# Layer norms of a two-block network: statistics about the first group's mean, scale and shift folded into the operand, output stored by column blocks

## The reference

```python
for i in range(2):
    sh, sc, gt = modulation(c_lat, w_ada[i], b_ada[i], 3)   # cond vector times a 2048 x 6144 matrix
    u = x * (1.0 + sc) + sh
    y = even_mixer(u, ...) if i == 0 else odd_mixer(u, ...)  # end in "@ w_out", 2048 x 2048
    x = layer_norm_2(alpha * x + gt * y, ln_g[i], ln_b[i])   # alpha = 4 ** 0.25
return x

def layer_norm_2(x, g, b):
    mu = mean(x, -1); var = mean((x - mu) ** 2, -1)          # over the 2048 channels of a token
    return (x - mu) * rsqrt(var + 1e-5) * g + b
```

## Time and profile before

| | us |
|---|---|
| median of 3 runs | 3116.04 (3108.94 to 3119.6) |
| the profiled execution, whole | 3112.09 |
| its span, first to last instruction | 3110.3 |
| TensorE busy | 2884.9 (93%) |
| VectorE busy | 1744.7 (56%) |
| ScalarE busy | 1024.1 (33%) |
| DMA, mean over the span | 145 GB/s |

### The profile page before, as it was taken

One profiled execution on the slowest core, in us unless ns is written; L12 is line 12 of the kernel. 1 busy time (PEld: TensorE's weight loads), 2 busy tenths in 40 slices (PEclk: granted clock), 3 DMA queues, 4 the chain that ended last, 5 costly groups with the idle time before them and its releaser, 6 DMA issues.

```text
span 3110.3 us, 36197 instructions
## 1 busy us (share of the span) xinstructions
PE 2884.9 (93%) x12539; PEld 2245.0 (72%) x12539; DVE 1744.7 (56%) x2683; ACT 1024.1 (33%) x1583; POOL 15.8 (1%) x26
## 2 busy tenths in 40 slices
PE   6999999989999979599999999999999699999995
PEld 3478877666788757378878777776788488888883
DVE  6855764444687555354427466473866576325343
ACT  3032223333332253322234435342322332234224
POOL 0000000000000000000000000000000000000000
PEclk9999999999999989799999999999999899999997
DMA  9975642212466346165522222233666274333331
GB/s 348 336 224 189 190 142 79 61 58 68 136 203 204 132 152 235 61 221 189 191 80 89 75 81 75 81 101 117 208 218 214 73 249 147 95 96 101 122 109 54
DMA packets 225492, 451.14 MB, mean 145 GB/s; under 512 B 23752, under 2 KB 29338, under 8 KB 221004
## 3 DMA queue, kind: packets, MB, share of 16 engines
q1 hardware_dynamic: 222548, 440.80, 43.2%
q0 software_dynamic: 2304, 8.39, 0.8%
q10 hardware_dynamic: 504, 0.17, 0.0%
HBM read 422.01 MB, written 27.30 MB: 144 GB/s over the span
## 4 chain that ended last, share of the span: by engine, by line
PE 83%; DVE 5%; ACT 4%; issue 2%; DMA 2%; DVEq 1%; ACTq 1%; SPq 1%; PEldq 0%; PEld 0%
PE ps L1142 20%; PE ps L1144 20%; PE ps L1143 20%; PE ps L1234 4%; PE ps L1151 2%; PE ps L1153 2%; PE ps L1152 2%; PE ps L1512 2%; PE ps L1195 2%; PE ps L1382 1%; DMA a_raw<-in_w_ada 1%; PE ps L1390 1%; PE ps L1121 1%; PE ps L1543 1%; PE ps L1546 1%
## 5 line engine op out<-in xcount | busy, mean ns | idle before, releaser
L1142 PE MATMUL ps<-op_hi,w_hi 128*128 128x512 f32 (+2 forms) x2928 | 1174.4, 401 | 56.4 <-DVE op_lo L1676 17.9
L1143 PE MATMUL ps<-op_lo,w_hi 128*128 128x512 f32 (+2 forms) x2928 | 1152.2, 394 | 0.0
L1144 PE MATMUL ps<-op_hi,w_lo 128*128 128x512 f32 (+2 forms) x2928 | 1152.1, 393 | 0.0
L1570 DVE TENSOR_TENSOR w_lo<-w_raw,w_hi 128x512 fp32r<-128x512 f32 (+2 forms) x640 | 421.4, 661 | 597.7 <-ACT w_hi L658 391.4
L1142 PEld LDWEIGHTS ps<-op_hi,w_hi 128*128 128x128 f32 (+1 forms) x2928 | 559.0, 191 | 193.3 <-issue 28.4
L1144 PEld LDWEIGHTS ps<-op_hi,w_lo 128*128 128x128 f32 (+1 forms) x2928 | 558.2, 191 | 119.1
L1143 PEld LDWEIGHTS ps<-op_lo,w_hi 128*128 128x128 f32 (+1 forms) x2928 | 559.7, 191 | 112.3 <-issue 1.9
L658 ACT ACTIVATE w_hi<-w_raw 128x512 fp32r<-128x512 f32 x464 | 292.5, 632 | 905.0 <-PE ps L1144 732.3
L1593 DVE SCALAR_TENSOR_TENSOR acc<-a_raw,vec,acc 128x512 f32<-128x512 f32 x525 | 381.7, 746 | 22.8 <-DMA a_raw<-in_w_ada 22.8
L634 ACT ACTIVATE w_hi<-w_raw 128x512 fp32r<-128x512 f32 (+2 forms) x240 | 134.5, 565 | 357.0 <-PE ps L1144 301.9
L1151 PE MATMUL ps<-w_hi,op_hi 128*128 128x512 f32 x384 | 152.6, 397 | 14.5 <-DVE w_lo L1570 14.5
(11 more groups left out here) (221 smaller groups left out, 2331.9 us busy)
## 6 DMA issues: line engine op xcount, KB each, us to landing
a_raw<-in_w_ada SPq DMA_DIRECT2D x216, 512.0 KB, 4.0
w_raw<-in_w_in_e SPq DMA_DIRECT2D x160, 512.0 KB, 4.6
w_raw<-in_w_in SPq DMA_DIRECT2D x96, 512.0 KB, 4.8
arena<-in_w_ada SPq DMA_DIRECT2D x72, 512.0 KB, 7.1
w_raw<-in_w_in_o SPq DMA_DIRECT2D x64, 512.0 KB, 3.8
w_raw<-in_w_out SPq DMA_DIRECT2D x32, 512.0 KB, 4.9
w_raw<-in_w_out_e SPq DMA_DIRECT2D x32, 512.0 KB, 4.9
w_raw<-in_w_out_o SPq DMA_DIRECT2D x32, 512.0 KB, 3.6
```

Source lines behind the costliest of these rows:

```text
L1142: mm(dst, hi[:, cols], B.op_hi[:, k, 0:tok], start=first, stop=False)
L1143: mm(dst, hi[:, cols], B.op_lo[:, k, 0:tok], start=False, stop=False)
L1144: last = mm(dst, lo[:, cols], B.op_hi[:, k, 0:tok], start=False, stop=last_t)
L1570: V.tensor_tensor(B.w_lo[:, c % RING, 0:width], B.w_raw[:, c // 2 % RAW, c % 2, 0:width], B.w_hi[:, c % RING, 0:width].bitcast(f32), ALU.s ...
```

## The change

- **Statistics beside the groups.** When `wo2` 0 (and `wo3` 0) is evacuated, its four tiles are added and summed on TensorE during group 1 (one ones-product at t = 3). The mean of those 512 channels per token, negated, is the shift. At t = 5 VectorE adds it to tiles 0 to 3; the residuals of groups 1 to 3 get it when they are scaled, now at t = 13 of their group, so all of Y is held about that mean. During group i (1 to 3) ScalarE squares the four tiles of group i - 1 and VectorE adds the tiles and the squares into sums. After group 3 only its own four tiles are left: TensorE adds the stored sum and four tiles, and the stored squares and four tiles' squares, ten ones-products, and the variance is E[y^2] - E[y]^2.
- **No centring pass.** A tile is normed by a multiply with the inverse deviation r and a subtraction of mean * r.
- **Folding.** For the operand of `xp`, gain, bias, scale and shift are combined into one scale and one shift per channel, so ScalarE makes the operand from the normed tile by one Identity. Gain and bias of the stream itself are applied one tile at a time, four tiles behind the operand (`stream_gain`), the last four after tile 15.
- **Output.** The end goes by blocks of 512 channels: gains of block j + 1, then copies of block j, one store of [512 tokens x 512 channels] per block from four buffers.
- The last three modulation parts move from `xp` 0 to 2 to `xp` 1 to 3. ScalarE's loops over `wo2` and `wo3` groups, and VectorE's over `wo3` groups, are written out step by step.

Core of the diff (hunks for bookkeeping left out; blank lines too):

```diff
     part = 8
     for start, count in ((first["f"], 7), (first["gb"], 5), (first["ck"], 2), (first["r"], 6),
-                         (first["egb"] + 1, 8)):
+                         (first["egb"] + 1, 5), (first["xp"] + 1, 3)):
...
+SHIFT_AT, SHIFTED_AT, SQUARED_AT, SCALED_AT = 3, 5, 9, 13
...
-    for t in range(NT):
-        sp.wait_ge(sem("out_rows"), t + 1)
-        sp.dma_start(B.out[0, t * P:(t + 1) * P, :], at(AT_OUT, 2, D)[:, t % 2, :]).then_inc(sem(f"out_done_{t % 2}"), 16)
-    for k in range(2):
-        sp.wait_ge(sem(f"out_done_{k}"), 16 * NT // 2)
+    for j in range(4):
+        sp.wait_ge(sem("out_rows"), j + 1)
+        cols = slice(j * GC, (j + 1) * GC)
+        sp.dma_start(B.out[0].rearrange("(t p) d -> p t d", p=P)[:, :, cols], at(AT_OUT, NT, D)[:, :, cols])\
+            .then_inc(sem("out_done"), 16)
+    sp.wait_ge(sem("out_done"), 64)
...
+    def group_squares(n, t):
+        g = GROUPS[n]
+        if g["name"] not in ("wo2", "wo3") or t != (SHIFTED_AT + 2 if g["i"] == 1 else SHIFTED_AT) or not g["i"]:
+            return
+        k, j = ("wo2", "wo3").index(g["name"]), g["i"] - 1
+        act.wait_ge(sem("centred"), 7 * k + j + 1)
+        if j:
+            act.wait_ge(sem("squares_added"), 3 * k + j)
+        Act(at(AT_SQ, 2048), Y[:, 4 * j:4 * j + 4, :].rearrange("p a b -> p (a b)"),
+            ACT.Square).then_inc(sem("tile_squared"), 1)
...
+    def last_squares(k):
+        act.wait_ge(sem("squares_added"), 3 * k + 3)
+        for t in range(4):
+            act.wait_ge(sem("centred"), 7 * k + 4 + t)
+            Act(at(AT_SQ, 4, S)[:, t, :], Y[:, 12 + t, :], ACT.Square).then_inc(sem("tile_squared"), 1)
...
+    def deviation(k):
+        act.wait_ge(sem("variance"), k + 3)
+        r = at(AT_RSTD, S)
+        Act(r, r, ACT.Ln, bias=B.eps[:, 0:1])
+        nc.scalar.drain()
+        Act(r, r, ACT.Exp, scale=-0.5).then_inc(sem("deviation"), 1)
...
+    def stream_gain(k, t):
+        g, b = (VEC[v] + 16 * k + t for v in ("ln_g", "ln_b"))
+        return Act(Y[:, t, :], Y[:, t, :], ACT.Identity, scale=B.vec[:, g:g + 1], bias=B.vec[:, b:b + 1])
...
+    def normed_operand():
+        n = first_use(5)
+        act.wait_ge(sem("w_used"), GROUPS[n]["kc"])
+        for t in range(KT):
+            act.wait_ge(sem("tile_normed"), t + 1)
+            if t >= 4:
+                act.wait_ge(sem("op_tile"), KT * 5 + t - 3)
+            x = at(TMP, 4, S)[:, t % 4, :]
+            Act(x, Y[:, t, :], ACT.Identity, scale=B.mod[:, 112 + t:113 + t], bias=B.mod[:, 96 + t:97 + t])
+            nc.scalar.drain()
+            Act(B.op_hi[:, t, :], x, ACT.Copy).then_inc(sem("op_high"), 1)
+            if t >= 4:
+                if t - 4 < early(n):
+                    step(n, t - 4)
+                last = stream_gain(0, t - 4)
+                if t % 4 == 3:
+                    last.then_inc(sem("scaled"), 1)
+        for t in range(12, KT):
+            last = stream_gain(0, t)
         last.then_inc(sem("scaled"), 1)
...
+        if name in ("wo2", "wo3") and i == 3:
+            last_squares(name == "wo3")
+            deviation(name == "wo3")
         if name == "wo2" and i == 3:
-            norm(2, 1)
-            from_mod(5, m=2)
+            normed_operand()
...
+    def out_taken(j):
+        for t in range(NT):
+            k = 4 * j + t
             act.wait_ge(sem("out_turned"), k + 1)
-            if t >= 2 and j == 0:
-                act.wait_ge(sem(f"out_done_{t % 2}"), 16 * (t // 2))
-            Act(at(AT_OUT, 2, D)[:, t % 2, j * GC:(j + 1) * GC], ps[:, k % 4, :], ACT.Copy).then_inc(sem("out_taken"), 1)
+            Act(at(AT_OUT, NT, D)[:, t, j * GC:(j + 1) * GC], ps[:, OUT_BANK + k % 4, :], ACT.Copy)\
+                .then_inc(sem("out_taken"), 1)
         nc.scalar.drain().then_inc(sem("out_rows"), 1)
+    for j in range(4):
+        for t in range(4 * j, 4 * j + 4):
+            act.wait_ge(sem("tile_normed"), KT + t + 1)
+            last = stream_gain(1, t)
+        last.then_inc(sem("scaled"), 1)
+        if j:
+            out_taken(j - 1)
+    out_taken(3)
...
+            if g["name"] in ("wo2", "wo3") and g["i"] == 1 and t == SHIFT_AT:
+                pe.wait_ge(sem("shift_added"), ("wo2", "wo3").index(g["name"]) + 1)
+                mm(ps[:, 4 * ((n + 1) % 2) + 2, :], B.ones, at(AT_SUM, S), start=True, stop=True)\
+                    .then_inc(sem("shift_summed"), 1)
...
+    def last_sums(k):
+        n = FIRST[("wo2", "wo3")[k]] + 3
+        bank = 4 * ((n + 1) % 2)
+        pe.wait_ge(B.bank_free[(n - 1) % 2], (n - 1) // 2 + 1)
+        pe.wait_ge(sem("squares_added"), 3 * k + 3)
+        mm(ps[:, bank, :], B.ones, at(AT_SUM, S), start=True, stop=False)
+        mm(ps[:, bank + 1, :], B.ones, at(AT_QSUM, S), start=True, stop=False)
+        for t in range(4):
+            pe.wait_ge(sem("centred"), 7 * k + 4 + t)
+            last = mm(ps[:, bank, :], B.ones, Y[:, 12 + t, :], start=False, stop=t == 3)
+            if t == 3:
+                last.then_inc(sem("summed"), 1)
+            pe.wait_ge(sem("tile_squared"), 7 * k + 4 + t)
+            last = mm(ps[:, bank + 1, :], B.ones, at(AT_SQ, 4, S)[:, t, :], start=False, stop=t == 3)
+        last.then_inc(sem("squares_summed"), 1)
...
+    def residual_scaled(k, i):
+        x = at(AT_XRES, 4, S)
+        dve.wait_ge(sem("residual_in"), 16 * (4 * k + i + 1))
+        if not i:
+            V.tensor_scalar(x, x, ALPHA, None, ALU.mult)
+        else:
+            V.scalar_tensor_tensor(out=x, in0=x, scalar=ALPHA, in1=at(AT_SHIFT, 1, S).to_broadcast([P, 4, S]),
+                                   op0=ALU.mult, op1=ALU.add)
+        V.drain()
+    def add_tiles(sums, x, first=False):
+        s = at(sums, 2, S)
+        if first:
+            V.tensor_tensor(s, x[:, 0:2, :], x[:, 2:4, :], ALU.add)
+        else:
+            V.tensor_tensor(s, s, x[:, 0:2, :], ALU.add)
+            V.drain()
+            V.tensor_tensor(s, s, x[:, 2:4, :], ALU.add)
+        V.drain()
+    def add_pair(sums):
+        s = at(sums, 2, S)
+        V.tensor_tensor(s[:, 0, :], s[:, 0, :], s[:, 1, :], ALU.add)
+    def statistics_beside(n, t):
+        g = GROUPS[n]
+        if g["name"] not in ("wo2", "wo3"):
+            return
+        k, i = ("wo2", "wo3").index(g["name"]), g["i"]
+        if i == 1 and t == SHIFTED_AT:
+            shift, y = at(AT_SHIFT, 1, S), Y[:, 0:4, :]
+            dve.wait_ge(sem("shift_summed"), k + 1)
+            V.tensor_scalar(shift[:, 0, :], ps[:, 4 * ((n + 1) % 2) + 2, :], -1.0 / GC, None, ALU.mult)
+            V.drain().then_inc(sem("shift_taken"), 1)
+            V.tensor_tensor(y, y, shift.to_broadcast([P, 4, S]), ALU.add)
+            V.drain().then_inc(sem("centred"), 1)
+            add_tiles(AT_SUM, y, True)
+        if i and t == SQUARED_AT:
+            dve.wait_ge(sem("tile_squared"), 7 * k + i)
+            add_tiles(AT_QSUM, at(AT_SQ, 4, S), i == 1)
+            if i == 3:
+                add_pair(AT_SUM)
+                add_pair(AT_QSUM)
+            V.drain().then_inc(sem("squares_added"), 1)
+            if i == 3 and not k:
+                b, gain = (B.vec[:, VEC[v]:VEC[v] + 16] for v in ("ln_b", "ln_g"))
+                shift, scale = B.mod[:, 96:112], B.mod[:, 112:128]
+                V.tensor_tensor(B.small[:, 72:88], b, scale, ALU.mult)
+                V.drain()
+                V.tensor_tensor(shift, shift, B.small[:, 72:88], ALU.add)
+                V.tensor_tensor(scale, scale, gain, ALU.mult)
+                V.drain()
+        if t == SCALED_AT:
+            residual_scaled(k + 1, i)
+    def statistics(k):
+        n = FIRST[("wo2", "wo3")[k]] + 3
+        bank = 4 * ((n + 1) % 2)
+        mean, msq, r = (at(w, S) for w in (AT_MEAN, AT_MSQ, AT_RSTD))
+        dve.wait_ge(sem("summed"), k + 1)
+        V.tensor_scalar(mean, ps[:, bank, :], 1.0 / D, None, ALU.mult)
+        V.drain()
+        V.tensor_tensor(msq, mean, mean, ALU.mult)
+        V.drain()
+        dve.wait_ge(sem("squares_summed"), 8 + k + 1)
+        V.scalar_tensor_tensor(out=r, in0=ps[:, bank + 1, :], scalar=1.0 / D, in1=msq,
+                               op0=ALU.mult, op1=ALU.subtract).then_inc(sem("variance"), 1)
+        dve.wait_ge(sem("deviation"), k + 3)
+        V.tensor_tensor(at(AT_MR, S), mean, r, ALU.mult)
+        V.drain()
+    def norm_tiles(first, count):
+        y = Y[:, first:first + count, :]
+        V.tensor_tensor(y, y, at(AT_RSTD, 1, S).to_broadcast([P, count, S]), ALU.mult)
+        V.drain()
+        V.tensor_tensor(y, y, at(AT_MR, 1, S).to_broadcast([P, count, S]), ALU.subtract)
+        V.drain().then_inc(sem("tile_normed"), count)
+    def normed_operand():
+        n = first_use(5)
+        norm_tiles(0, 1)
+        norm_tiles(1, 1)
+        for p in range(KT // 2):
+            for t in (2 * p, 2 * p + 1):
+                dve.wait_ge(sem("op_high"), KT * 5 + t + 1)
+                split_lo(t, at(TMP, 4, S)[:, t % 4, :])
+                if t % 2 == 0 and p + 1 < KT // 2:
```

(52 more changed lines are left out.)

78 lines of the change are left out of this document (26 added, 52 removed).

## The result

| | before | after |
|---|---|---|
| median, us | 3114.18 (3108.94 to 3119.6, 4 runs) | 3083.03 (3079.51 to 3083.62, 4 runs) |
| span of the profiled execution | 3110.3 | 3080.7 |
| start to the last product of `wo2` | 2428.8 | 2430.9 |
| last product of `wo2` to that of `wo3` ("middle" below) | 617.7 | 603.76 |
| last product of `wo3` to the end ("tail") | 63.8 | 46.0 |

The ratio of the times is 0.9897, with a 95% interval from 0.9878 to 0.9917: some 31 us faster, where 30 were forecast (3086, range 3073 to 3100). The span fell by 29.6 us, and the sum of the terms said 29.8. Stages matter more here than whole times: single executions of one kernel differ by 1 to 12 us. In the profiles of kernels that are alike up to the last product of `wo2` that product ends anywhere from 2427 to 2436 us.

The account below looks back on a forecast made before the run. TensorE bounds the kernel, so time is won only at the two norms. 13.7 + 17.8 - 1.7 = 29.8 us off the profiled 3112.09 gave 3082.3; with the median 4 higher, 3086 us, range 3073 to 3100.

Parts of the forecast that it names:

- Ones-product at 0.86: Both norms' sums on TensorE: one ones-product of 512 columns takes 0.86 us at 2.4 GHz; the other end is 1.72.
- bridge A: Norm of `wo2`, its last product to `xp`'s first, 46.3 us before: 27.9 us shorter, of which `xp` 1 gains 13.7.
- rival 2: Slow statistics: ones-products at 1.2 GHz (+6.9 per norm) or ScalarE slower than TensorE; 3093 to 3100 us; chance 0.19.
- First product of `xp` 18.5 after `wo2`'s last: Across the norm of `wo2`: `xp`'s first product at 2447.3 where it was 2475.16, 27.9 us earlier.
- `xp` 0 in 45.9 us: First group of `xp`: its products end at about 2493.2, 45.9 us after its start, operand making just under TensorE's pace.
- Last gain 45.8 after Exp: During `xp` 0: ScalarE's 16 operand tiles plus four gains end about 45.8 us after 2442.7, at 2488.5.
- The store holds `xp` 1's weights: 4 MB store waits for all 16 gains, ahead of these weights; TensorE stands 11.9 us, slow restart 2.6 more.
- Tail 46.0: From `wo3`'s last product to the end: 46 us where it was 63.8, 17.8 us less.
- Added work costs nothing: Groups 1 to 3 of `wo2` and `wo3`: VectorE's added blocks, largest 5.8 us, stay under 8.2 us of lead.
- Moving the parts costs nothing: Modulation part from `xp` 0 to `xp` 3: 0.66 us per tile leaves VectorE in one, enters the other; cost 0.
- Rival 1: The store at `xp` 1 holds nobody up: bridge A gives 26 to 28 us; time 3072 to 3074; chance 0.13.
- rivals 3 and 4: Gain lost at `xp` 1 and tail, 3107 to 3116, chance 0.06; VectorE becomes bound in `wo2`/`wo3`, 3118 to 3125, 0.04.

Follow-up runs that it names:

- e7: Changed kernel with the ten last ones-products of each norm held until the last square is there: 3093.55 us (2 runs), ratio 0.9927 to before.
- e1: Changed kernel without the 4 MB store of the stream, so its output isn't the reference's: 3072.45 us, ratio 0.9871 to before.
- e2: Changed kernel with the 4 MB store cut into four of 1 MB, each behind its four gains and ahead of one `xp` 1 weight pair: 3076.72 us.
- e3: Changed kernel with the whole 4 MB store moved behind the first four weight pairs of `xp` 1: 3076.37 us, ratio 0.9883 to before.
- e8: Changed kernel with three more 2048-column additions (7.03 us) in VectorE's block at t = 5 of `wo2` 1 and `wo3` 1: 3096.66 us.
- e4: Changed kernel with the three modulation parts back on `xp` 0 to 2: 3092.1 us, ratio 0.9927 to before.
- e10: Changed kernel with the store in quarters and, in both norms, the mean taken off tiles 0 to 3 during Ln and Exp: 3070.46 us.

## Why the prediction was right, step by step

- **Bounds.** Time was won only at the two norms, as read from the earlier trace rows. The change of the middle and the tail, 13.9 + 17.7, is all of it and 2 us more; 2.1 were lost before `wo2`'s end, of which 0.86 is the shift's product and the rest no more than this stage differs by from run to run (2427 to 2436 in the runs with nothing changed there). That the sum came within 0.2 of the span's change is in part luck: the middle gave 1.1 more than was said, and this stage 1.2 less. The forecast of the time also started from a median of 3116.04, where the four runs give 3114.18.
- **Ones-product at 0.86.** Confirmed: 0.86 each in the chain, clock 1.00. e7 shows what later sums, partly at 1.2 GHz, would have cost: 7.1 in bridge A, 5.7 in the tail; rival 2 had 6.9 a bridge.
- **First product of `xp` 18.5 after `wo2`'s last.** 19.0. The Y sums ended 0.2 later and each of the small steps took a few hundredths more.
- **`xp` 0 in 45.9 us.** It took 47.4, so this term was 1.5 too low. Its own parts don't give 45.9 either: 16 tiles of 2.72 are 43.5, and 2 before tile 4 and 2.6 of slow clock would make it 48.1. Measured beside the 43.5: no wait of TensorE at all, 2.7 in 13 records at 0.50, and 0.9 for eight small products of a modulation part (L1184, 2469.00 to 2469.80), which no term has. The 2.6 was misread too: the earlier trace rows has 15 records in 5.0 us at `xp`'s start before, 1.5 lost. ScalarE's pace, 2.63 a tile, was right (2.60).
- **Last gain 45.8 after Exp.** 46.4: Exp ended at 2445.1, the last gain at 2491.5. ScalarE stood 1.7 and 1.8 us for normed pairs before tiles 2 and 4, and then never again.
- **The store holds `xp` 1's weights.** Confirmed by e1, e2 and e3. The stall was 9.4 instead of 11.9. Of the difference, 2.0 are `xp` 0's later end (0.5 from its start, 1.5 from its length); the rest is the store, which landed in 12.4 and not 13.8, less what the last gain was late. `xp` 1 started 75.9 us after `wo2`'s last product, and 76.3 were forecast. What was lost behind the stall was 2.1 (2.6 said).
- **Bridge A in all.** 13.7 less 0.86 for the shift was said, and 13.9 measured for the middle. How the 27.3 us that its chain lost divide among the sums made beside the groups, the missing centring pass and the folding is read from the chain alone; no run takes them apart.
- **Tail 46.0.** 46.0, but by two errors that cancel. Exp ended 12.7 after the last product (12.6 said), the last tile was normed at 35.1 (34.5). The last copy was out at 40.8 (41.6 said): I had the transposes at the low clock as the limit of the last block, but there they ran at 2.4 GHz (16 records in 2.03 us from 3071.90 on), and it was ScalarE's eight copies back to back, 4.21. From the last copy to the end it was 5.3, not 4.4: the store of 2 KB rows landed in 4.5 in the median, not 3.9, inside my bound of 6.
- **Added work costs nothing.** Right for `wo2` and `wo3`: no wait in either but two short ones for w_lo at the start of `wo2`, 2.5 in all, where before has 2.4. e8 puts the cover at 9.4 to 10.4 us.
- **Moving the parts costs nothing.** Right against the kernel before, but it misses what the move is for: with the new order, leaving them would have cost 8.3 (e4). I had followed the weights past the store in SP's queue and not the part's loads.
- **Rivals.** Rival 1 (no one is held, 3072 to 3074) describes e1's 3072.45 well, so its price was right and its condition false. Rival 2 did not come about: the sums ran at 1.00 and ScalarE kept up. Nor did rivals 3 and 4.

## What to carry to other kernels

When a stage gets shorter, look at each queue for what now waits on its last result, and at what stands behind it: here a store that must wait for the whole of a tensor held the next group's weights, and cutting it in four pieces that leave earlier gave back 11.3 of the 11.5 us, moving it whole behind four pairs of weights 9.2. Two edits that look independent can be worth more together: spreading copies between gains pays once the gains come with gaps, and hardly before. And where an engine works a list in program order, moving one operation earlier doesn't help if the one that is waited for still stands behind others (e10 in bridge A).
